# A seventh place for expert weights in a transformer block kernel: kept residuals, spent probability rows, and the order of the weight queue

## The chip, the cores and the metric

The kernel runs on one core of a Trainium2 chip (trn2). The metric is the device time of one execution in microseconds (us). The program is one hand-written instruction stream for each engine: PE (TensorE), DVE (VectorE), ACT (ScalarE), POOL (GpSimd) and SP (SyncE), which in this kernel issues most of the DMAs. The engines meet at semaphores only.

## The reference

One layer on x of 512 tokens by 1024 channels, all in float32, in three parts, each added to the residual x, and a final norm:

```python
h = rmsnorm(x, norm_mix_g);  x = x + parallel_mixers(h, ...)          # windowed attention and gated DeltaNet
h = rmsnorm(x, norm_x_g);    x = x + memory_cross_attention(h, m, ...) # 4 heads of 128, 256 memory tokens
h = rmsnorm(x, norm_ffn_g);  x = x + hierarchical_moe(h, ...)
return rmsnorm(x, norm_final_g)

# hierarchical_moe: top 1 of 4 groups, top 2 of 8 experts in it
for e in range(32):                                   # D_MODEL 1024, D_EXPERT 256
    hid = silu(t @ w_exp_gate[e]) * (t @ w_exp_up[e])
    out = out + combine[:, e:e + 1] * (hid @ w_exp_down[e])
```

The gate, up and down weights of one expert are 1024 by 256, 1024 by 256 and 256 by 1024 floats: three pieces of 1024 KB each, 96 pieces for the 32 experts.

## The kernel before, in words

The first two parts (to about 550 us of the span) are a list of jobs, `job_order()`. Every engine walks the same list and does its share of each job: PE the matmuls of a job into one of eight PSUM banks, ACT or DVE the emptying of the bank. `job_done(eng, job)` waits until PE has done a job, `job_empty(eng, job)` until its bank is emptied. `LATE_BANKS` gives fixed banks to the last jobs, and a bank is only overwritten when the job before in it was emptied. The jobs that matter here stand at the end of cross-attention and in the routing:

- `("xv", t)`: output of tile t of the attention (128 tokens). Its high part goes to `h_hi`, its low part (the rest that the rounding of the high part leaves) to `h_lo`, by a subtraction on VectorE. `("co", t, n)` multiplies both with the halves n of `w_co` and adds into the residual `xres`.
- `("rt", t)`, `("pos", t)`: router and the places of the tokens in each expert's list. `("g0", t)` gathers expert 0's rows by matmul, `("ls",)` makes the lists of rows for all experts, `("gt",)` turns expert 0's rows, `("most",)` counts the longest list.
- `("kr", h)`: a matmul with the identity that copies half a residual tile (tile 2) into PSUM, as the start of a sum.

Then comes the expert loop. Each expert has up to 64 token slots. For each, PE does: `gate_up` (64 matmuls, `bank<-arena,hT`, L1424), the turning of the next expert's gathered rows (L1411), the transpose of the hidden rows (L1446) and `down_rows` (8 matmuls, L1434). Then ACT empties the bank (L1737), and POOL scatters the rows to `y_half` in memory (L990). POOL also gathers the rows of the experts ahead (L985). Expert 31's rows are not scattered but added by matmul. After expert 30's scatter has landed, SP reads all of `y_half` back (L847, 8 reads), the tiles are summed (tiles 0 and 1 on DVE, tiles 2 and 3 in PSUM, L1507), normed and stored.

The weights live in six slots (`UNROLL`), each with a place for gate, up and down: slots 0 to 4 in the `arena` (a buffer of 32768 words for each partition) and slot 5 in the `ring` of the earlier weight chunks. Slot 2 takes words 12288 to 18431, slot 3 words 18432 to 24575, slot 4 words 24576 to 30719. The upper half of the arena is also `h_hi` (16384), `h_lo` (20480), `w_high` (24576) and `w_low` (28672), 4096 words each, while the first two parts run. So slot 3's up weights (words 20480 to 22527) lie on the first half of `h_lo`, where the low parts of the output stand until the last `co` job.

All weights are issued by SP, in one order written out by hand: the pieces of experts 0 to 5 by `load_part(b, i)` (i is 0 gate, 1 up, 2 down) between the chunks and behind `job_done` waits, and from expert 6 on by `load_expert`. That waits until the weights of the expert two before have landed (`w_loaded`, L818), until the slot's gate and up were used (`gu_done`, L819) and, ahead of the down piece, until its down was used (`down_done`, L822). The order in the queue is gate, up, down of one expert, then those of the next.

Tile 3's residual is copied to PSUM in the expert loop, behind expert 25's down (`KEEP_AT`, `keep_residual`, L1459), since `sum_banks(3)` are banks 2 and 3. The final norm's gains are loaded to the arena's last 1024 words (L841).

## Time and profile before

| what | value |
|---|---|
| time, median of 3 runs | 829.1 us (828.96 to 829.15) |
| the profiled execution | 829.2 us |
| its span, first to last instruction | 827.4 us |
| granted TensorE clock, mean | 0.994 of full speed |
| busy: PE / PE weight loads / DVE / ACT / POOL | 775.1 / 623.0 / 343.8 / 239.2 / 312.3 us |
| moved by DMA | 166.95 MB, mean 202 GB/s |
| queue of SP (q1) | 150.66 MB |
| waits of SP for landed up weights (L818), 480 us to the end | 154.7 us in 22 waits |

The page cuts the span into 40 slices of 20.7 us. All times in the rows below are microseconds from the start of the span; the profiled execution's own time is 1.8 us longer than its span. In a timeline row the first number is the start, the second the duration; x64 means that 64 instructions were merged; what stands in brackets is idle time of the engine before it, and what ended that. PEld is TensorE's weight load, SPq a DMA issue of SP.

### The profile page before, as it was taken

The numbers are of one execution on the slowest core, as the hardware profiler recorded it, in microseconds if no ns is written. First come the engines' busy times: TensorE is split into PE (matmuls) and PEld (weight loads), VectorE is DVE, ScalarE is ACT, GpSimd is POOL, SyncE is SP. The second block draws the span as 40 slices with busy tenths as digits, with TensorE's granted clock in tenths as the row PEclk, the third lists the DMA queues.
The fourth block names the chain that finished last, engine by engine and source line by source line (L and its number), as shares of the span: only waits on it lengthen the run. The fifth ranks groups of instructions, "written<-read, shape, count | busy, mean of one in ns | idle before, by whom it ended". The sixth has DMA issues, their size and how long they took to land.

```text
span 827.4 us, 14485 instructions
## 1 busy us (share of the span) xinstructions
PE 775.1 (94%) x5739; PEld 623.0 (75%) x5739; DVE 343.8 (42%) x767; ACT 239.2 (29%) x417; POOL 312.3 (38%) x354
## 2 busy tenths in 40 slices
PE   5999999999999999999999999998999999988785
PEld 5987788888988877788888887866777777756651
DVE  6466651474575484325512624372222221121126
ACT  5344242112221458632222445331111111110012
POOL 3774434542242244143542454334333333322111
PEclk9999999999999999999999999999999999999998
DMA  9956832402202232446478255679999999999976
GB/s 250 167 108 119 266 66 55 98 2 52 51 1 53 51 102 52 94 102 187 81 157 229 70 173 183 254 282 343 388 388 388 390 387 383 392 386 381 390 299 250
DMA packets 74347, 166.95 MB, mean 202 GB/s; under 512 B 18838, under 2 KB 46310, under 8 KB 66344
## 3 DMA queue, kind: packets, MB, share of 16 engines
q1 hardware_dynamic: 65856, 150.66, 57.7%
q0 software_dynamic: 5392, 9.61, 3.5%
q10 hardware_dynamic: 3032, 5.74, 2.2%
q8 instruction: 47, 0.77, 0.4%
q14 instruction: 20, 0.16, 0.1%
HBM read 157.31 MB, written 16.97 MB: 211 GB/s over the span
## 4 chain that ended last, share of the span: by engine, by line
PE 64%; DMA 25%; DVE 4%; POOL 2%; issue 2%; ACT 2%; SPq 1%; DVEq 0%; POOLq 0%; ACTq 0%
DMA arena<-in_w_exp_up 23%; PE bank L1067 15%; PE bank L1074 13%; PE bank L1076 13%; PE bank L1075 13%; PE bank L1424 2%; DMA arena<-y_half 1%; PE bank L1434 1%; PE bank L1115 1%; PE bank L1225 1%; PE bank L1167 1%; POOL w_low L889 1%; PE bank L1279 1%; POOL xres L927 1%; PE bank L1411 1%
## 5 line engine op out<-in xcount | busy, mean ns | idle before, releaser
L869 POOL TENSOR_TENSOR ring_low<-ring,w_high 128x512 fp32r<-128x512 f32 (+1 forms) x64 | 83.6, 1306 | 124.7 <-ACT w_high L1516 120.7
L1074 PE MATMUL bank<-h_hi,w_high 128*128 128x512 f32 x296 | 122.1, 412 | 0.9 <-ACT arena L1630 0.9
L1075 PE MATMUL bank<-h_lo,w_high 128*128 128x512 f32 x296 | 115.8, 391 | 0.0
L1424 PEld LDWEIGHTS bank<-arena,hT 128*64 128x64 f32 x1728 | 96.6, 136 | 24.1 <-issue 12.5
L1424 PE MATMUL bank<-arena,hT 128*64 128x128 f32 x1728 | 100.7, 274 | 8.2 <-DMA arena<-in_w_exp_up 6.1
L869 POOL TENSOR_TENSOR w_low<-ring,w_high 128x512 fp32r<-128x512 f32 x56 | 75.1, 1341 | 59.9 <-ACT w_high L1516 55.8
L2142 DVE SCALAR_TENSOR_TENSOR rt<-rt,bank 128x128 f32<-128x128 f32 x32 | 9.2, 288 | 175.2 <-ACT rt L1733 175.2
L1516 ACT ACTIVATE w_high<-ring 128x2048 fp32r<-128x2048 f32 (+1 forms) x32 | 58.9, 1839 | 57.1 <-PE bank L1076 37.2
L1074 PEld LDWEIGHTS bank<-h_hi,w_high 128*128 128x128 f32 x296 | 55.7, 188 | 15.2 <-issue 3.5
L1076 PE MATMUL bank<-h_hi,ring_low 128*128 128x512 f32 x168 | 66.1, 393 | 0.0
L1075 PEld LDWEIGHTS bank<-h_lo,w_high 128*128 128x128 f32 x296 | 55.7, 188 | 9.5
L1434 PE MATMUL bank<-arena,rt 128*64 128x512 f32 x216 | 52.3, 605 | 10.3 <-DVE rt L2146 10.3
L990 POOL DMA_INDIRECT y_half<-rows,cst x31 | 31.7, 1021 | 74.0 <-ACT rows L1737 73.2
L1074 PE MATMUL bank<-w_high,h_hi 128*128 128x512 f32 (+1 forms) x144 | 52.6, 365 | 0.5 <-DVE h_lo L2041 0.5
L1076 PE MATMUL bank<-w_high,h_lo 128*128 128x512 f32 (+1 forms) x144 | 51.2, 356 | 0.0
L1737 ACT ACTIVATE rows<-bank 128x512 f32<-128x512 f32 x32 | 19.1, 598 | 108.6 <-PE bank L1434 108.6
L1076 PE MATMUL bank<-h_hi,w_low 128*128 128x512 f32 x128 | 49.9, 390 | 0.0
L1075 PE MATMUL bank<-w_low,h_hi 128*128 128x512 f32 (+1 forms) x128 | 44.8, 350 | 0.0
L1733 ACT ACTIVATE rt<-bank 128x128 f32<-128x128 f32 x32 | 8.9, 278 | 108.2 <-PE bank L1424 105.3
L985 POOL DMA_INDIRECT hT<-h_rows,rt x31 | 30.5, 982 | 24.5 <-POOL rt L980 23.7
L1076 PEld LDWEIGHTS bank<-h_hi,ring_low 128*128 128x128 f32 x168 | 31.5, 188 | 7.4
L1516 ACT ACTIVATE arena<-bank 128x512 f32<-128x512 f32 (+1 forms) x39 | 23.3, 597 | 46.4 <-PE bank L1076 26.1
(325 smaller groups left out, 1368.7 us busy)
## 6 DMA issues: line engine op xcount, KB each, us to landing
arena<-in_w_exp_gate SPq DMA_DIRECT2D x27, 1024.0 KB
arena<-in_w_exp_up SPq DMA_DIRECT2D x27, 1024.0 KB
arena<-in_w_exp_down SPq DMA_DIRECT2D x27, 1024.0 KB
ring<-in_w_in SPq DMA_DIRECT2D x33, 512.0 KB, 6.7
ring<-in_w_exp_gate SPq DMA_DIRECT2D x5, 1024.0 KB
ring<-in_w_exp_up SPq DMA_DIRECT2D x5, 1024.0 KB
ring<-in_w_exp_down SPq DMA_DIRECT2D x5, 1024.0 KB
xres<-in_x SPq DMA_DIRECT2D x8, 512.0 KB, 7.3
```

Source lines behind the costliest of these rows:

```text
L869: after(pool.tensor_tensor(low, full, high, ALU.subtract), w_lo if kk == KD - 2 else step["pool"])
L985: pool.indirect_dma_start(out=xg[:, b % DEEP, :], out_offset=None, in_=h_rows, in_offset=bass.IndirectOffsetOnAxis(ap=idx[b][0:CAP, :], ax ...
L990: pool.indirect_dma_start(out=y_half, out_offset=bass.IndirectOffsetOnAxis(ap=at_y, axis=0), in_=ysb[:, y, :], in_offset=None, bounds_chec ...
L1067: ins = pe.matmul(o, l, r, start=(n == 0), stop=(n == len(pairs) - 1))
L1074: pe.matmul(o, l_hi, r_hi, start=(n == 0), stop=False)
L1075: pe.matmul(o, l_hi, r_lo, start=False, stop=False)
L1076: ins = pe.matmul(o, l_lo, r_hi, start=False, stop=(n == count - 1))
L1424: ins = pe.matmul(bank[CAP * half:CAP * half + CAP, 1, P * n:P * n + P], xgT[:, x, kk, :], w[:, kk, P * half:P * half + P], start=(kk == 0 ...
L1434: ins = pe.matmul(bank[CAP * half:CAP * half + CAP, o, :], hidT[:, CAP * kk:CAP * kk + CAP], down[:, kk, 512 * half:512 * half + 512], sta ...
L1516: after(nc.scalar.activation(o, i, ACT.Copy, scale=scale), s)
L1737: nc.scalar.activation(ysb[:, y, :], bank[:, 4 + b % 2, :], ACT.Copy).then_inc(y_sb, 1)
L2142: nc.vector.scalar_tensor_tensor(out=gated, in0=gate_th, scalar=1.0, in1=bank[:, 1, 0:P], op0=ALU.add, op1=ALU.mult).then_inc(step["dve"], 1)
```

## The change

- The low parts of the attention's output go to `out_lo`: the second halves of the rows of `hT` in which the probabilities of tile t stood, which `xv` no longer needs. `h_lo` is free from then on, so slot 3's up piece is issued together with its gate and down.
- Gate and up weights get seven places (`GATES = 7`), used in turn by e % 7; down weights keep six, used by e % 6. The seventh gate is in the arena's last 2048 words, the seventh up in `xres` of tiles 2 and 3.
- For that the residual of tile 3 too is copied to PSUM ahead of the expert loop: jobs `("k3", 0)` and `("k3", 1)`, banks 2 and 3, between `g0` and `ls`. `ls` moves from bank 3 to bank 5. The copy in the expert loop goes away.
- SP issues expert 6's gate right behind slot 4, its up after `k3`; and from expert 7 on the order is gate and up of expert e, then down of expert e - 1. `gu_done` is waited for one expert less, `e + 1 - 7`.
- The rows of `y_half` are read back to words 22528 to 30719 of the arena, and the final gains are loaded only after 29 experts' downs.

```diff
-KEEP_AT = {26: 3}
+GATES = UNROLL + 1
...
-    jobs += [("g0", 0), ("g0", 1), ("pos", 3), ("g0", 2), ("g0", 3), ("ls",), ("gt",), ("most",)]
+    jobs += [("g0", 0), ("g0", 1), ("pos", 3), ("g0", 2), ("g0", 3), ("k3", 0), ("k3", 1), ("ls",), ("gt",), ("most",)]
...
-LATE_BANKS = {"g0": 0, "gt": 0, "ls": 3, "most": 4, "kr": 6}
+LATE_BANKS = {"g0": 0, "gt": 0, "k3": 2, "ls": 5, "most": 4, "kr": 6}
+KEPT = ("kr", "k3")
...
+        x_row_parts = y_hi[:, :, :].rearrange("p k t -> p (k t)")
+        out_lo = [x_row_parts[:, D * t + 512:D * t + D].rearrange("p (k l) -> p k l", k=4) for t in range(NT)]
...
         def y_rows(t, j):
-            first = 2 * EW + (2 * t + j) * D
+            first = (UNROLL - 2) * EW - 2 * D + (2 * t + j) * D
...
+            n = e % GATES
+            if n < UNROLL:
+                gate, up = home(n)[:, 0:KD * FE], home(n)[:, KD * FE:2 * KD * FE]
+            else:
+                gate, up = arena[:, arena_words - KD * FE:arena_words], xres[:, 2:NT, :].rearrange("p t d -> p (t d)")
+            return [gate.rearrange("p (k f) -> p k f", k=KD), up.rearrange("p (k f) -> p k f", k=KD),
+                    home(e % UNROLL)[:, 2 * KD * FE:EW].rearrange("p (k n) -> p k n", k=2)]
...
             job_done(sp, ("cq", X_HEADS - 1))
-            load_part(3, 0)
-            load_part(3, 2)
+            for i in range(3):
+                load_part(3, i)
...
             load_part(2, 2)
-            load_part(3, 1)
             sp.wait_ge(hrow_ready, NT)
             for i in range(3):
                 load_part(4, i)
...
-                sp.wait_ge(w_loaded[(b - 2) % UNROLL], i * 32 + (32 if b >= 2 else 0))
+            load_gate(GATES - 1)
+            job_done(sp, ("k3", 1))
+            load_up(GATES - 1)
+            for e in range(GATES, EXPERTS):
+                sp.wait_ge(w_loaded[(e - 2) % UNROLL], 32 * ((e - 2) // UNROLL) + 32)
                 sp.sem_inc(loading, 1)
-                sp.wait_ge(gu_done, i * UNROLL + (b + 1 - UNROLL))
...
+                sp.wait_ge(gu_done, e + 1 - GATES)
+                load_gate(e)
+                load_up(e)
+                load_down(e - 1)
+            load_down(LAST_EXPERT)
...
+            sp.wait_ge(down_done, EXPERTS - 3)
             sp.dma_start(gain_out, norm_final_g.rearrange("(o d) -> o d", o=1).to_broadcast([P, D])).then_inc(gains_in, 16)
-            sp.wait_ge(down_done, EXPERTS - 4)
...
-                    return split_sums(o, [(h_parts(kk, slice(t * P, (t + 1) * P)), w_parts(c0, kk, 0, 512, 4)) for kk in range(4)])
+                    return split_sums(o, [(out_parts(kk, t), w_parts(c0, kk, 0, 512, 4)) for kk in range(4)])
...
-                if e1 in KEEP_AT:
-                    keep_residual(KEEP_AT[e1])
...
-                    after(tt(h_lo[s], oh4, h_hi[s].bitcast(F32), ALU.subtract), e)
+                    after(tt(out_lo[c], oh4, h_hi[s].bitcast(F32), ALU.subtract), e)
```

`load_down(e)` waits for `down_done` of `e + 1 - UNROLL`, six experts back, and issues that expert's down piece.

## Rows read from the trace of the kernel before

**Rows 1.** The page's slices of 20.7 us: GB/s moved by DMA.

```profile
GB/s 250 167 108 119 266 66 55 98 2 52 51 1 53 51 102 52 94 102 187 81 157 229 70 173 183 254 282 343 388 388 388 390 387 383 392 386 381 390 299 250
```

**Rows 2.** The page's chain that ended last: share of the span by line.

```profile
DMA arena<-in_w_exp_up 23%; PE bank L1067 15%; PE bank L1074 13%; PE bank L1076 13%; PE bank L1075 13%; PE bank L1424 2%; DMA arena<-y_half 1%; PE bank L1434 1%; PE bank L1115 1%; PE bank L1225 1%; PE bank L1167 1%; POOL w_low L889 1%; PE bank L1279 1%; POOL xres L927 1%; PE bank L1411 1%
```

**Rows 3.** Timeline of TensorE in the expert loop: gate and up (L1424), down (L1434).

```profile
575.93 1.31 PE L1424 MATMUL bank<-arena,hT 128*64 128x128 f32 x20
...
720.01 3.72 PE L1424 MATMUL bank<-arena,hT 128*64 128x128 f32 x64
...
727.57 3.77 PE L1424 MATMUL bank<-ring,hT 128*64 128x128 f32 x64 [0.18 <-DMA ring<-in_w_exp_up]
...
789.45 3.77 PE L1424 MATMUL bank<-arena,hT 128*64 128x128 f32 x64 [0.51 <-DMA arena<-in_w_exp_up]
...
794.94 1.94 PE L1434 MATMUL bank<-arena,rt 128*64 128x512 f32 x8 [0.38 <-DVE rt L2146]
...
797.56 3.52 PEld L1424 LDWEIGHTS bank<-arena,hT 128*64 128x64 f32 x64 [0.34 <-DMA arena<-in_w_exp_up]
```

**Rows 4.** Timeline of SP's DMA issues; then two rows of the page's issues.

```profile
499.02 0.33 SPq L756 DMA_DIRECT2D arena<-in_w_exp_gate  x1
...
546.24 0.38 SPq L756 DMA_DIRECT2D arena<-in_w_exp_down  x1
...
551.32 0.33 SPq L756 DMA_DIRECT2D arena<-in_w_exp_gate  x1
...
563.02 0.33 SPq L821 DMA_DIRECT2D arena<-in_w_exp_gate  x1
...
572.47 0.33 SPq L821 DMA_DIRECT2D arena<-in_w_exp_gate  x1
...
arena<-in_w_exp_up SPq DMA_DIRECT2D x27, 1024.0 KB
...
h_rows<-hT POOLq DMA_DIRECT2D x3, 512.0 KB, 3.7
```

**Rows 5.** Windows: stretch, length, busy time by engine, clock, DMA share, GB/s.

```profile
508.20:518.00 9.80, 9.30 (x56) 7.83 (x55) 3.85 (x7) 6.44 (x11) 6.29 (x6) 1.00 0.01 3
...
545.90:551.30 5.40, 5.36 (x34) 3.87 (x34) 3.78 (x18) 2.47 (x4) 2.61 (x9) 1.00 0.95 340
551.30:562.70 11.40, 8.88 (x121) 6.44 (x118) 7.44 (x39) 1.02 (x3) 2.82 (x9) 1.00 0.99 396
...
563.00:564.00 1.00, 0.00 (x0) 0.00 (x0) 0.47 (x2) 0.28 (x1) 0.80 (x2) 1.00 0.22 45
564.00:565.00 1.00, 0.46 (x3) 0.27 (x5) 0.39 (x2) 0.00 (x0) 0.41 (x1) 1.00 0.94 143
```

**Rows 6.** Timeline: tile 3's residual copy, the lists' matmuls, POOL before the first gather.

```profile
752.27 1.98 PE L1459 MATMUL bank<-xres,cst 128*128 128x512 f32 x4
754.18 2.07 PE L1424 MATMUL bank<-arena,hT 128*64 128x128 f32 x33
...
556.39 1.07 PE L1372 MATMUL bank<-cst 128*64 128x32 f32 x32
...
559.20 0.42 POOL L980 COPY rt<-rt 64x1 int32<-64x1 int32 x2 [3.56 <-DMA h_rows<-rows]
```

**Rows 7.** The chain that ended last, from expert 30's scatter on: start, duration.

```profile
798.31 4.06 DMA y_half<-rows,cst
...
806.11 9.97 DMA arena<-y_half
```

**Rows 8.** DMA queues over 564 to 604, over 801 to 802; gathers' landing times.

```profile
q1 hardware_dynamic: 2349, 13.44, 89.6%
...
q0 software_dynamic: 9, 0.02, 4.3%
q1 hardware_dynamic: 4, 0.01, 3.1%
...
DMA to landing us min/median/max: 6.6/7.1/7.4
```

More of the change, by code:

```diff
@@ L812, in _, with load_gate, load_up, load_down @@
                 load_part(4, i)
-            def load_expert(i, b):
-                parts, sources = expert_parts(b), expert_sources(i * UNROLL + b)
-                sp.wait_ge(w_loaded[(b - 2) % UNROLL], i * 32 + (32 if b >= 2 else 0))
-                sp.sem_inc(loading, 1)
-                sp.wait_ge(gu_done, i * UNROLL + (b + 1 - UNROLL))
-                for n in range(2):
-                    sp.dma_start(parts[n], sources[n]).then_inc(w_loaded[b], 16)
-                sp.wait_ge(down_done, i * UNROLL + (b + 1 - UNROLL))
-                sp.dma_start(parts[2], sources[2]).then_inc(down_loaded[b], 16)
-            for i in range(1, TURNS):
-                for b in range(UNROLL):
-                    load_expert(i, b)
-            for b in range(REST):
-                load_expert(TURNS, b)
+            def load_gate(e):
+                sp.dma_start(expert_parts(e)[0], expert_sources(e)[0]).then_inc(w_loaded[e % UNROLL], 16)
+            def load_up(e):
+                sp.dma_start(expert_parts(e)[1], expert_sources(e)[1]).then_inc(w_loaded[e % UNROLL], 16)
+            def load_down(e):
+                sp.wait_ge(down_done, e + 1 - UNROLL)
+                sp.dma_start(expert_parts(e)[2], expert_sources(e)[2]).then_inc(down_loaded[e % UNROLL], 16)
+            load_gate(GATES - 1)
[3 more added lines that the diff above has]
+                sp.wait_ge(w_loaded[(e - 2) % UNROLL], 32 * ((e - 2) // UNROLL) + 32)
+                sp.sem_inc(loading, 1)
+                sp.wait_ge(gu_done, e + 1 - GATES)
[3 more added lines that the diff above has]
+            load_down(LAST_EXPERT)
             most = sp.value_load(most_i[0:1, :], min_val=0, max_val=T)
@@ L1387, in emit @@
                     return ins
[L1388 to L1390 removed]
+                if k in KEPT:
+                    t = 2 + KEPT.index(k)
+                    job_empty(pe, ("co", t, job[1]))
+                    return pe.matmul(o, ident, xres[:, t, 512 * job[1]:512 * job[1] + 512], start=True, stop=False, skip_group_check=True)
                 if k == "most":
@@ L1396, in _ @@
             for n, job in enumerate(jobs):
-                if before_in_bank[job] and before_in_bank[job][0] not in PARTIAL + ("kr",):
+                if before_in_bank[job] and before_in_bank[job][0] not in PARTIAL + KEPT:
                     job_empty(pe, before_in_bank[job])
@@ L1416, in turn_rows, with gate_up @@
                 turn(b, turned)
-            def gate_up(b, x, s):
-                gate, up, _ = expert_parts(b)
+            def gate_up(e, x, s):
+                gate, up, _ = expert_parts(e)
                 for kk in range(KD):
@@ L1452, in expert @@
                     turn_next()
-                if e1 in KEEP_AT:
-                    keep_residual(KEEP_AT[e1])
-            def keep_residual(t):
-                for half in range(2):
-                    pe.matmul(sum_banks(t)[:, half, :], ident, xres[:, t, 512 * half:512 * half + 512], start=True, stop=False, skip_group_check=True)
             pe.sem_inc(turning, 1)
```

19 lines of the change are left out of this document (8 added, 11 removed).

## The prediction

> **What bounds the kernel now.** I read the page's row of slices first: from about 580 us to the end of the experts the DMA engines move some 390 GB/s, slice after slice, and no slice shows more; before 500 us the rate swings between nearly nothing and 270, and only then climbs [rows 1]. The chain of work that ended last then gives 23% of the span to landings of up weights, more than to any other line [rows 2]. The timeline of TensorE shows when that wait is real. An expert's gate and up matmuls start every 7.20 us from 575.93 to 720.01 (20 experts, no wait), so in that stretch TensorE sets its own pace and weights pile up ahead of it; from 727.57 on they start late, released by weights, and the gate of expert 30, which TensorE alone could have begun at 575.93 + 28 x 7.20 = 777.5, begins at 789.45 [rows 3]. So the last nine experts, and with them the end, go by the weight stream: a microsecond by which the stream is ahead at 600 us is one by which it is ahead at 790, as the engines are never idle between (the rate stays at 380 to 395) [rows 1]. TensorE has 12 us to spare. What an edit is worth is therefore: how much earlier does the stream reach the piece that the end waits for, and which piece is that.
>
> **What runs ahead of the stream.** SP issues all weights into one queue, so a piece lands in its place in the order. Slot 3's gate and down go out at 499.02, slot 5 and most of slot 2 from 518 on; slot 2's down goes at 546.24 with slot 3's up right behind it, slot 4 at 551.32, and expert 6's gate at 563.02, as soon as expert 0's gate and up matmuls let slot 0 go [rows 4]. Between, the engines idle: from 508.2 to 518 they move 3 GB/s, and after slot 4 there is a hole around 563 to 565 (45 and 143 GB/s) [rows 5].
>
> **Part 1, slot 3's up goes out with its gate.** The low parts of the output move from h_lo to rows of hT whose probabilities are spent, so one piece, 1024 KB or 1.05 MB [rows 4], leaves the stretch after 546 and falls into the idle 508 to 518: at 396 GB/s, the rate of 551.3 to 562.7 [rows 5], that is 2.65 us, costing nothing before (2.65 us fit into 9.8 idle ones). The subtraction on VectorE and the matmuls keep shape and count: 0. But slot 4 still waits for the last normed row, to 551.32. From 545.9 to 551.3 the engines moved 340 x 5.4 = 1.84 MB [rows 5]; without the piece there is only a row store of 0.52 MB [rows 4] and 1.05 of slot 2's down in that queue, 1.57, so it runs dry 0.27 MB, or 0.7 us, before 551.3: at 550.6. A load takes time to flow: in the 2 us after the issue at 563.02 only 0.19 MB moved, worth 0.5 us, so 1.5 are lost [rows 4, 5]. Slot 4 flows from 551.3 + 1.5 = 552.8. A new hole of 2.2 us; net gain 2.65 - 2.2 = 0.45.
>
> **Part 2, the seventh gate and up.** They are issued right behind slot 4, before expert 0 has run, and close the old hole: the queue was dry at 562.7 and flowed again at 563.0 + 1.5 = 564.5, 1.8 us. So the stream is ahead by 0.45 + 1.8 = 2.25, say 2.3 us. Not by the 5.3 us that two pieces of 1.05 MB take: the stream can gain only time in which it stood still. The bounds: if slot 4 follows without a hole of its own, 2.65 + 1.8 = 4.5; if the new hole is as large as the piece and latency is 1 us, 0 + 1.3 = 1.3.
>
> **Part 3, tile 3's residual moves ahead of expert 0.** The same four matmuls took from 752.27 to the next start at 754.18, 1.9 us, in a place where the weights were late anyway [rows 3, 6]; taking them away there gives 0. In their new place, between the first gather's sums and the slot lists, TensorE has no idle time (the lists' matmuls begin at 556.39 with no wait) [rows 6], so lists, first gate and all experts start 1.9 us later. TensorE's 12 us of slack cover that at the end. What is late next is the issue of gate 7 (564.9 instead of 563.0), of down 6 behind expert 0's down, and of gate 8 (572.47 + 1.9 = 574.4) [rows 4]. Queued then: slot 4 until 562.2, after it five pieces, 5.24 MB; the queue's own rate among gathers is 13.44 MB in 40 us, 336 GB/s [rows 8], so 15.6 us, to 577.8. It isn't dry at 574.4: 3.4 us of cover, and 0 for this part. Without that cover it would cost up to 1.9. The gathers wait for the lists too; the last row store already held them to 559.20 [rows 6], so they lose under 1.2 us. The ls bank (5) was emptied by then.
>
> **Part 4, the order of the pieces.** Before: gate, up, down of one expert. After: gate 31, up 31, then down 30, down 31. In mid-stream nothing changes. At the end the critical step is expert 30's down: its result must be scattered to memory and read back, and the chain goes from its start at 794.94 to the last read at 816.09 [rows 3, 7]. It began 5.5 us after up 30 landed, and its own weights, the next piece, were there by then. Now down 30 stands last but one in the queue, the place of up 31 before, and up 31 was waited for to 797.56 [rows 3]. So without a gain down 30 would start at 797.5: a loss of 2.6 us (bounds 2.3, as the weight load was held only the last 0.34 us, and 2.9, one piece of 2.65 us behind a down that comes late by 0.3). With 2.3 us of lead it starts at 795.2, +0.3 to now. TensorE could start it at: down 29 in up 30's old place, 789.4 - 2.3 = 787.1, plus 1.9 for it, 3.7 for gate and up, 1.7 for hidden: 794.4, so the weights decide.
>
> **Part 5, the scatter behind it.** It took 4.06 us from 798.31 [rows 7], with weights still in the engines: between 801 and 802 nine of its packets ran beside four of the weight queue [rows 8]. Now the weights end 2.3 us before it: those nine come with the others. I take 0.7 us off, between 0 (it is bound by its own start and end) and 1.4 (all the time after 801). By the Trainium skill (DMA: Bandwidth & Descriptors, Anatomy of one DMA) such a transfer takes about 2.0 us plus bytes over 436 GB/s; for 128 rows of 2 KB that is 2.6 us, against 4.06 in the trace, and by it the gain would be 1.4 and the sum 828.0 in place of 828.7. The first gathers contend as before. The final gains load (0.5 MB) is issued after expert 28 instead of at the last weights: it stays behind down 31 in the queue, and nothing asks for it before the tiles are summed: 0. Reads of y into other words of the arena: 0, their slots are free after expert 28, and SP waits for the scatter far longer.
>
> **Sum.** On the profiled 829.2: order +2.6, lead -2.3, scatter -0.7, rest 0: 828.8; against the median of 829.1 that is 828.7. Its own range, with the lead at 1.8 to 3.0 and the scatter at 0.3 to 1.2, is 827.4 to 829.6. About 0.2%, 1.7 us, is what a measurement here tells from no change.
>
> **Rivals.**
> (a) The lead is larger than the holes I count: slot 4 without a new hole (the piece in front still fills the time, as row stores drag) gives 4.5, and the scatter 1.0: 829.1 + 2.6 - 4.5 - 1.0 = 826.2; with the low order cost 825.9. For it: the rate of 545.9 to 551.3 is only 340, so something slows pieces there. Against it: the engines' share is 0.95 in it, so they are held, not idle [rows 5], and SP issues at fixed waits. It is over the bound from a lead of 3.6. Chance 0.28.
> (b) Slower: expert 0's delay of 1.9 us becomes a hole. If queue time is shorter than I think, or the first gathers land late (they take 6.6 to 7.4 us) [rows 8], SP stands at gate 8 or down 7 with an empty queue. Lead 2.3 - 1.9 = 0.4, order +2.6, scatter 0: 829.1 + 2.2 = 831.3. It decides from a lead plus scatter under 0.9. For it: down 6 and the first gathers all fall in the 10 us behind the gate at 563.02, where SP's waits and TensorE's steps stand closest [rows 4]. Against it: the 3.4 us of cover. Chance 0.2.
> (c) The seventh place does nothing for the stream because the w_loaded wait (two experts back) limits it. Then lead 0.45 and order 2.6: 830.6 after the scatter; this is within the bound. In the trace that wait first binds past 600 us. It shares the 0.52 of the middle with my forecast, 0.07 of it.
>
> **Numbers.** Forecast 0.45 and (c) 0.07 make 0.52 within 0.2%; (a) 0.28 faster; (b) 0.20 slower. The range goes from (a)'s 826.2 to just short of (b)'s, 831.0.
>
> **What would show it.** In the new profile: SP issues slot 3's up near 499.4 and the engines are busy to 511; a hole at 550.6 to 552.8 and none at 563 (step 1, 2); the first expert's gate 1.9 us later (3); past 740 us TensorE waits in front of L1434's down matmuls for in_w_exp_down, no more for in_w_exp_up, and expert 30's down starts near 795.2 (4); scatter to landing near 3.4 us (5). Wrong it would be if the last down 30 landed more than 1.5 us off 795.2, or if a second hole stood between 565 and 600.

## Result and the profile after

The changed kernel takes 831.03 us (median of 20 executions, 829.2 to 834.1) against 829.18 for the kernel before (20 executions on the same chip, 828.5 to 830.7): a ratio of 1.0023 with a 95% interval of 1.0016 to 1.0029. It is 1.9 us slower; I had forecast 828.7 with 831.0 as the upper end and gave "slower" 2 chances in 10. The profiled execution took 829.5 us (span 827.6), which is at the fast end of the changed kernel's executions, so its trace shows the places of the loss and not its full size. The executions also scatter more than before (standard deviation 1.25 us against 0.62), and their mean granted TensorE clock lies between 0.981 and 0.991: the lower the clock, the longer the execution as a rule (correlation -0.65 over the 20).

The page's slices and chain, which answer to [rows 1] and [rows 2]: the slices after 580 us look the same, and the chain now has landings of down weights in it, which it had not.

```profile
GB/s 250 167 108 120 265 67 54 100 1 52 51 2 52 51 102 52 95 101 186 81 151 231 73 172 234 254 227 365 374 389 379 396 389 385 388 386 389 392 289 248
...
DMA arena<-in_w_exp_up 16%; PE bank L1080 15%; PE bank L1087 13%; PE bank L1089 13%; PE bank L1088 13%; DMA xres<-in_w_exp_up 4%; PE bank L1441 3%; DMA arena<-in_w_exp_down 2%; DMA ring<-in_w_exp_up 2%; PE bank L1451 1%; PE bank L1517 1%; PE bank L1131 1%; PE bank L1241 1%; DVE h_lo L1830 1%; PE bank L1295 1%
```

SP's issues (timeline of SP; to be held against [rows 4]) and windows of the changed kernel (against [rows 5]; columns as there):

```profile
499.60 0.43 SPq L765 DMA_DIRECT2D arena<-in_w_exp_up  x1
...
551.60 0.33 SPq L765 DMA_DIRECT2D arena<-in_w_exp_gate  x1
...
558.79 0.33 SPq L826 DMA_DIRECT2D xres<-in_w_exp_up  x1
...
578.91 0.33 SPq L823 DMA_DIRECT2D arena<-in_w_exp_gate  x1
```

```profile
508.20:518.00 9.80, 9.30 (x56) 7.84 (x56) 3.92 (x8) 6.65 (x11) 6.16 (x5) 1.00 0.27 110
...
551.30:554.00 2.70, 1.61 (x8) 0.29 (x4) 2.23 (x13) 0.27 (x1) 0.33 (x1) 1.00 0.38 52
...
563.00:565.00 2.00, 2.00 (x41) 2.00 (x39) 1.32 (x8) 0.00 (x0) 1.19 (x3) 1.00 1.03 426
...
579.00:581.00 2.00, 1.62 (x11) 1.10 (x12) 1.31 (x4) 0.20 (x1) 0.23 (x2) 1.00 0.82 158
```

Slot 3's up goes out at 499.60 and falls into the idle stretch (110 GB/s where 3 were). The old hole at 563 is closed (426 GB/s). The new hole that I had placed at 550.6 to 552.8 stands at 551.3 to 554, with 52 GB/s. A second one, which I had ruled out and named as a sign of being wrong, stands at 579 to 581 (158 GB/s). Gate 8, which waits for expert 1's gate and up to be used, goes out at 578.91, where I had written 574.4. In the kernel before, the issue that waited for the same matmuls was gate 7's, at 572.47.

TensorE's timeline shows why, and then the late experts (k3's copy is L1407, lists L1388, gate and up L1441, turn L1428, down L1451; against [rows 3, 6]):

```profile
556.77 1.98 PE L1407 MATMUL bank<-xres,cst 128*128 128x512 f32 x4
558.69 1.12 PE L1388 MATMUL bank<-cst 128*64 128x32 f32 x32
...
561.60 3.74 PE L1441 MATMUL bank<-arena,hT 128*64 128x128 f32 x64 [1.06 <-DVE hT L2104]
...
567.40 3.53 PE L1451 MATMUL bank<-arena,rt 128*64 128x512 f32 x8 [0.38 <-DVE rt L2156]
571.54 1.07 PE L1428 MATMUL bank<-cst,hT 64*128 64x64 f32 x8 [0.61 <-DMA hT<-h_rows,rt]
573.48 5.40 PE L1441 MATMUL bank<-arena,hT 128*64 128x128 f32 x64 [0.87 <-DMA arena<-in_w_exp_up]
...
762.87 3.26 PE L1451 MATMUL bank<-arena,rt 128*64 128x512 f32 x8 [2.43 <-DMA arena<-in_w_exp_down]
...
781.17 1.94 PE L1451 MATMUL bank<-arena,rt 128*64 128x512 f32 x8 [2.69 <-DMA arena<-in_w_exp_down]
...
788.64 1.94 PE L1451 MATMUL bank<-ring,rt 128*64 128x512 f32 x8 [0.68 <-DMA ring<-in_w_exp_down]
790.38 3.71 PE L1441 MATMUL bank<-arena,hT 128*64 128x128 f32 x64
...
796.60 1.94 PE L1451 MATMUL bank<-arena,rt 128*64 128x512 f32 x8 [1.17 <-DMA arena<-in_w_exp_down]
```

Expert 0's gate comes 2.35 us later than before (561.60 against 559.25), of which 0.28 stood already when slot 4 was issued (551.60 against 551.32); the copy itself pushes it by 2.07. Its down matmuls take 3.53 us where they took 1.94, and expert 1's gate and up 5.40 where they took 3.74. (The wait in brackets there is put down to up weights, but the same 0.88 us stands there in the kernel before, released by VectorE.) Those are the stretches with half the granted clock, 1.2 instead of 2.4 GHz:

```profile
568.00:571.00 3.00, 2.93 (x8) 0.49 (x4) 0.00 (x0) 0.03 (x1) 0.00 (x0) 0.50 0.99 268
574.50:577.50 3.00, 3.00 (x32) 3.00 (x31) 0.00 (x0) 0.00 (x0) 1.33 (x3) 0.50 0.99 404
```

The turn of expert 1 (571.54) waits for gathers, which take longer now (landing times of the gathers issued in 555 to 575; in the kernel before they are 7.2/7.3/7.4 in the same window):

```profile
DMA to landing us min/median/max: 6.7/9.1/9.4
```

At the other end the waits in front of gate and up have turned into waits in front of down. Expert 30's down starts at 796.60 (before 794.94; I had written 795.2). The chain of the end, start and duration, and below it the timeline of the scatter (L1003) and the reads (L860), against [rows 7]:

```profile
778.64 17.82 DMA arena<-in_w_exp_down
796.60 1.94 PE bank L1451 x8
799.13 3.71 PE bank L1441 x64
```

```profile
799.96 0.99 POOL L1003 DMA_INDIRECT y_half<-rows,cst  x1 [6.78 <-ACT rows L1747]
...
802.42 4.22 SPq L860 DMA_DIRECT2D arena<-y_half  x8
```

From the scatter's start to the first read it is 2.46 us, where it was 4.13 (798.31 to 802.44). So the reads start at 802.42, as early as before, although expert 30's down is 1.7 us later.

### The profile page after: what moved, and what is told of

Same layout as the page of the kernel before. It is cut to its first block, busy times and chain, and to the rows that moved or that the text cites. A ratio compares the mean times of both kernels' runs of the same rounds, so it can differ in the third digit from the quotient of the medians.

```text
span 827.6 us, 14484 instructions
## 1 busy us (share of the span) xinstructions
PE 777.7 (94%) x5739; PEld 626.4 (76%) x5739; DVE 344.6 (42%) x767; ACT 239.6 (29%) x417; POOL 310.2 (37%) x354
## 4 chain that ended last, share of the span: by engine, by line
PE 65%; DMA 24%; DVE 5%; ACT 2%; POOL 1%; issue 1%; SPq 1%; DVEq 0%; ACTq 0%; POOLq 0%
DMA arena<-in_w_exp_up 16%; PE bank L1080 15%; PE bank L1087 13%; PE bank L1089 13%; PE bank L1088 13%; DMA xres<-in_w_exp_up 4%; PE bank L1441 3%; DMA arena<-in_w_exp_down 2%; DMA ring<-in_w_exp_up 2%; PE bank L1451 1%; PE bank L1517 1%; PE bank L1131 1%; PE bank L1241 1%; DVE h_lo L1830 1%; PE bank L1295 1%
## 5 line engine op out<-in xcount | busy, mean ns | idle before, releaser
L882 POOL TENSOR_TENSOR ring_low<-ring,w_high 128x512 fp32r<-128x512 f32 (+1 forms) x64 | 81.7, 1277 | 126.6 <-ACT w_high L1526 122.7
L1441 PEld LDWEIGHTS bank<-arena,hT 128*64 128x64 f32 x1664 | 97.9, 138 | 17.0 <-issue 16.0
L1441 PE MATMUL bank<-arena,hT 128*64 128x128 f32 x1664 | 104.9, 276 | 1.9 <-DVE hT L2104 1.1
L1451 PE MATMUL bank<-arena,rt 128*64 128x512 f32 x216 | 55.2, 634 | 15.9 <-DVE rt L2156 8.4
L1003 POOL DMA_INDIRECT y_half<-rows,cst x31 | 31.7, 1021 | 76.6 <-ACT rows L1747 75.7
L1451 PEld LDWEIGHTS bank<-arena,rt 128*64 128x64 f32 x216 | 14.0, 141 | 37.3 <-issue 21.8
L1089 PE MATMUL bank<-w_high,h_lo 128*128 128x512 f32 (+1 forms) x112 | 38.7, 345 | 0.0
```

Of the source, the lines that this page charges most:

```text
L882: after(pool.tensor_tensor(low, full, high, ALU.subtract), w_lo if kk == KD - 2 else step["pool"])
L1003: pool.indirect_dma_start(out=y_half, out_offset=bass.IndirectOffsetOnAxis(ap=at_y, axis=0), in_=ysb[:, y, :], in_offset=None, bounds_chec ...
L1089: ins = pe.matmul(o, l_lo, r_hi, start=False, stop=(n == count - 1))
L1441: ins = pe.matmul(bank[CAP * half:CAP * half + CAP, 1, P * n:P * n + P], xgT[:, x, kk, :], w[:, kk, P * half:P * half + P], start=(kk == 0 ...
L1451: ins = pe.matmul(bank[CAP * half:CAP * half + CAP, o, :], hidT[:, CAP * kk:CAP * kk + CAP], down[:, kk, 512 * half:512 * half + 512], sta ...
```

## Experiments

Each was run beside the kernel before on the same chip, and the ratio is to that kernel. "Interval" is the 95% one. A trace is of one execution, which can lie over 2 us from the median; where it does, I say so.

**1. The old order from expert 16 on, the rest as changed.**

```diff
                 load_gate(e)
                 load_up(e)
-                load_down(e - 1)
-            load_down(LAST_EXPERT)
+                if e <= 16:
+                    load_down(e - 1)
+                if e >= 16:
+                    load_down(e)
```

> The changed kernel, but from expert 16 on the queue has the old order again (gate, up, down of one expert); the seventh place stays. Theory A (the order at the end costs what the lead gains: in the profile of the changed kernel expert 30's down waits for its weights until 796.6): the critical down starts 5.5 us after up 30, which now lands in down 29's place less one piece, near 788.3, so at 793.9 in place of 796.6, and the time falls by 2 to 2.7 us against the changed kernel, to about 828.5, faster than the kernel before by 0.1%. Theory B (the order is free, all of the loss is made ahead of 600 us by late gathers and the low clock): no change to the changed kernel, 831.0.

Measured: 829.63 us, 1.0006, interval 0.9997 to 1.0014. So the new order costs the changed kernel 1.4 us, and everything else in the change together is worth nothing, +0.5 us, where I had counted -2.3. The gain is real but short of theory A's 2 to 2.7 us. The trace is of the slowest of the 11 executions (830.96), so it can't show the gain: gate 30 starts at 790.99 and down 30 at 796.47. The early stage is as in the changed kernel, somewhat worse (timeline of TensorE; turn L1430, gate and up L1443), and 39 GB/s move over 579 to 581:

```profile
571.48 1.07 PE L1430 MATMUL bank<-cst,hT 64*128 64x64 f32 x8 [2.55 <-DMA hT<-h_rows,rt]
573.42 6.60 PE L1443 MATMUL bank<-arena,hT 128*64 128x128 f32 x64 [0.88 <-DMA arena<-in_w_exp_gate]
```

**2. Tile 3's copy behind expert 0's gate and up, the rest as changed** (up 6 then goes out behind gate and up 7).

```diff
-... ("g0", 3), ("k3", 0), ("k3", 1), ("ls",) ...
+... ("g0", 3), ("ls",) ...
-            job_done(sp, ("k3", 1))
-            load_up(GATES - 1)
...
+                if e == GATES:
+                    sp.wait_ge(kept, 1)
+                    load_up(GATES - 1)
...
                 gate_up(e1 - 1, b % 2, gu_done)
+                if e1 == 1:
+                    for half in range(2):
+                        ins = pe.matmul(sum_banks(3)[:, half, :], ident, xres[:, 3, 512 * half:512 * half + 512], start=True, stop=False, skip_group_check=True)
+                    ins.then_inc(kept, 1)
```

> The changed kernel, but tile 3's residual is copied to PSUM behind expert 0's gate and up, where TensorE idles 1.35 us for the hidden rows, and expert 6's up is issued behind expert 7's gate and up. Theory B (the copy on TensorE's path delays lists, gathers and expert 0, and with them SP's issues): first gate at 559.6 in place of 561.6, gate 8 issued 2 us earlier or more, the hole near 579 smaller, the time 1 to 2 us less than the changed kernel's 831.0. Theory A': the delay of the gathers comes from weights in front of them in the DMA engines, and not from the copy: turning of expert 1's rows stays near 571, gain under 0.5 us.

Measured: 829.84 us, 1.0016, interval 1.0005 to 1.0027. Expert 0's gate is back at 559.44, the gathers at 6.6/7.7/8.3 us, and in this trace expert 1's gate and up take 3.74 us at full clock; down 30 starts at 796.07. The clock is not the edit's doing, though: run 5 below has the same code up to expert 13, and there they take 5.40 us. Gate 8 goes out at 577.80, only 1.1 us earlier than in the changed kernel, as SP now waits 9.8 us for the landing of up 6, which stands further back in the queue. The time improves by 0.07% only, where theory B had 1 to 2 us, and the intervals do not tell it from nothing. What becomes of the rest isn't shown; the late stage of this trace has three down matmuls of 3.1 to 3.7 us in place of 1.94.

**3. The copy ahead of the lists alone**, on the kernel before (six places, old order, `ls` in bank 5).

```diff
-... ("g0", 3), ("ls",) ...
+... ("g0", 3), ("k3", 0), ("k3", 1), ("ls",) ...
-LATE_BANKS = {"g0": 0, "gt": 0, "ls": 3, "most": 4, "kr": 6}
+LATE_BANKS = {"g0": 0, "gt": 0, "k3": 2, "ls": 5, "most": 4, "kr": 6}
-KEEP_AT = {26: 3}
+KEEP_AT = {}
...
```

> The kernel before, but tile 3's residual is copied to PSUM ahead of the lists as in the changed kernel, and no longer behind expert 25; six places and the old order stay. Theory B: the stream waits for expert 0's gate, so SP's gate 6 goes out 1.9 to 2.3 us later, all of it shows at the end: 831.2, slower by 0.25%. Theory A: the stream makes good for it (no idle in the engines counts), within 0.5 us of 829.2.

Measured: 830.23 us, 1.0012, interval 1.0003 to 1.0021: 1.0 us for two microseconds of matmuls whose end I had priced at 0. Gate 0 starts at 561.31 (2.06 later), gate 6 goes out at 565.08 instead of 563.02, and down 30 starts at 797.62. Theory B had twice as much (+2.0 us).

**4. Slot 3's up early alone** (with the low parts in `out_lo`), on the kernel before.

```diff
-            load_part(3, 0)
-            load_part(3, 2)
+            for i in range(3):
+                load_part(3, i)
...
             load_part(2, 2)
-            load_part(3, 1)
```

> The kernel before with only the low parts of the output in the probability rows and slot 3's up issued with its gate; six places, old order, old residual copy. By my sum the piece brings 2.65 us and the new hole ahead of slot 4 takes 2.2 of it: 828.7, a gain of 0.45. The rival (no new hole, the piece in front drags) gives 2.6 us, 826.5. In the profile of the changed kernel the engines are empty from 551.0 to 553.6, which speaks for a hole of 2.6 and a gain near 0.

Measured: 828.34 us, 0.9987, interval 0.9978 to 0.9996: 1.1 us faster. Gate 30 starts at 788.94 and down 30 at 794.43, each 0.5 us earlier than before, as the sum of part 1 had it (0.45). The time gains more than that, but its interval reaches down to 0.3 us.

**5. Both repairs: old order from expert 13 on (as in 1, with 13 for 16), and the late copy (as in 2)**, seven places.

> The changed kernel with both repairs: tile 3's residual copied behind expert 0's gate and up (expert 6's up issued behind expert 7's), and the old order of the queue from expert 13 on. If the loss is made of the order at the end (1.4 us by the first pair of runs) and of the copy on TensorE's path (0.6 us), the two add up: 829.0 or less, near the low parts alone (828.3), and with the seventh place's own worth on top (a hole of 1.8 us closed) up to 827.5. Rival: the seventh place itself is worth nothing, as its loads stand in front of the first gathers: then no better than the low parts alone, 828.3.

Measured: 828.23 us, 0.9986, interval 0.9977 to 0.9994. Better than the changed kernel by 0.37%, but no better than part 1 alone: the seventh place, with the late copy that makes room for it, gives nothing here. Windows of part 1 alone (first fence) and of this kernel (second):

```profile
551.30:554.00 2.70, 1.43 (x8) 0.27 (x4) 2.24 (x13) 0.09 (x1) 0.14 (x1) 1.00 0.57 99
563.00:565.00 2.00, 0.45 (x5) 0.18 (x3) 0.86 (x3) 0.28 (x1) 1.20 (x3) 1.00 0.71 160
...
565.00:570.00 5.00, 4.12 (x38) 2.63 (x40) 0.69 (x1) 0.60 (x1) 1.28 (x4) 1.00 0.98 380
575.00:580.00 5.00, 5.00 (x73) 4.08 (x70) 0.00 (x0) 0.82 (x2) 1.81 (x3) 1.00 1.02 400
```

```profile
563.00:565.00 2.00, 2.00 (x10) 0.89 (x7) 0.57 (x2) 0.28 (x1) 1.20 (x3) 1.00 1.03 403
...
565.00:570.00 5.00, 3.35 (x18) 1.45 (x17) 0.70 (x2) 0.60 (x1) 0.45 (x2) 1.00 0.98 302
575.00:580.00 5.00, 4.62 (x46) 2.98 (x43) 1.46 (x4) 0.74 (x2) 1.36 (x3) 1.00 1.02 329
```

The hole at 563 is closed (403 against 160 GB/s over 2 us, 0.49 MB), but the stream gives it back: in 565 to 570 and 575 to 580 the engines are just as busy and move 0.39 and 0.36 MB less. From 546 to 605 us SP's queue moves 18.24 MB, and 18.38 in part 1 alone. Expert 1's gate and up take 5.40 us at low clock in this trace; but in run 2's, where they take 3.74, the same two stretches move 320 and 318 GB/s, so the loss is not the clock's.

**6. The new order alone**, on the kernel before (six places).

```diff
                 for n in range(2):
                     sp.dma_start(parts[n], sources[n]).then_inc(w_loaded[b], 16)
-                sp.wait_ge(down_done, i * UNROLL + (b + 1 - UNROLL))
-                sp.dma_start(parts[2], sources[2]).then_inc(down_loaded[b], 16)
+                e = i * UNROLL + b
+                if e > UNROLL:
+                    load_down(e - 1)
+                if e == LAST_EXPERT:
+                    load_down(e)
...
```

> The kernel before with only the new order of the queue from expert 7 on (down of an expert behind the next gate and up); six places, all else old. Theory A with the clock: expert 30's down waits for its weights at up 31's old place, 797.5 in place of 794.94, the scatter behind it shorter by 1.6: +1.0 us; and as TensorE now waits in front of down, its clock falls to 0.5 in some experts past 730 us, more than once an execution: mean clock 0.987 to 0.990 in place of 0.9956, spread of the runs 1.2 us in place of 0.6, in all +1.0 to +2.0 us, 830 to 831. Rival: the low clock comes from the early stage alone: clock 0.995, spread 0.6, +1.0 us at most.

Measured: 832.59 us (5 executions), 1.004, interval 1.0027 to 1.0053: 3.3 us slower. Timeline of TensorE at the end (gate and up L1431, down L1441):

```profile
755.00 3.59 PE L1441 MATMUL bank<-arena,rt 128*64 128x512 f32 x8 [1.77 <-DMA arena<-in_w_exp_down]
...
782.63 3.42 PE L1441 MATMUL bank<-arena,rt 128*64 128x512 f32 x8 [2.65 <-DMA arena<-in_w_exp_down]
...
791.31 1.94 PE L1441 MATMUL bank<-ring,rt 128*64 128x512 f32 x8 [0.38 <-DVE rt L2153]
798.52 1.94 PE L1441 MATMUL bank<-arena,rt 128*64 128x512 f32 x8 [0.38 <-DVE rt L2153]
```

Down 30 (798.52) waits for no weights: behind the wait of 2.65 us and a down of 3.42 us at low clock (0.72 over 782 to 788), TensorE goes at its own 7.2 us an expert to the end.

Not all of the 3.3 us is the order at the end. With six places the edit also moves down 6 behind gate 7 and up 7, which wait for expert 1, and so it opens an early hole (the window below moved 343 GB/s in the kernel before):

```profile
570.00:575.00 5.00, 4.62 (x58) 3.56 (x56) 1.46 (x4) 0.28 (x1) 1.84 (x3) 1.00 0.70 191
```

From 499 to 605 us SP's queue moves 26.46 MB against 27.19, which at 390 GB/s is 1.9 us. The changed kernel hasn't got this hole, so run 6 doesn't price the order in it.

**7. Slot 4's gate issued ahead of the wait for the last normed row**, on kernel 5.

```diff
             load_part(2, 2)
+            load_part(4, 0)
             sp.wait_ge(hrow_ready, NT)
-            for i in range(3):
+            for i in range(1, 3):
                 load_part(4, i)
```

> As the run with both repairs, and slot 4's gate is issued right behind slot 2's down, ahead of the wait for the last normed row, so that the queue doesn't run dry between 551 and 553.6. Theory: the stream is ahead by up to 2.6 us more, and the end with it, 1 to 2.6 us under the run with both repairs. Rival: the last row store and the first gathers wait behind that piece by as much, expert 1's rows are turned 2 us later, and SP loses at gate 8 what it won: no gain, within 0.5 us.

Measured: 827.10 us, 0.9974, interval 0.9964 to 0.9984; run again beside 13 below, 827.32 us, 0.9978, interval 0.9969 to 0.9987. It beats both kernels, by 2 us the one before and by nearly 4 the changed one. The windows show the hole of 551 filled, and the one of 563 open again (107 GB/s), since behind gate 6 nothing goes out before gate 7 at 563.1:

```profile
551.30:554.00 2.70, 1.42 (x8) 0.25 (x4) 2.24 (x13) 0.07 (x1) 0.13 (x1) 1.00 1.00 381
563.00:565.00 2.00, 2.00 (x7) 0.82 (x5) 0.57 (x2) 0.28 (x1) 1.20 (x3) 1.00 0.63 107
```

The gathers land after 6.8 us, expert 1's turn starts at 567.36 with no wait and its gate takes 3.74 us; gate 30 starts at 786.91, down 30 at 792.40.

**8. Matmuls in the waits**, on the changed kernel: three 128x128 matmuls in front of the wait for down weights, from expert 20 on, so that TensorE does not stand still there.

```diff
                 pe.wait_ge(y_sb, e1)
+                if e1 > 20:
+                    for _ in range(3):
+                        pe.matmul(bank[:, 4 + b % 2, 0:P], ident, ident, start=True, stop=True, skip_group_check=True)
                 pe.wait_ge(down_loaded[b], 16 * i + 16)
```

> The changed kernel with three small matmuls (128 by 128, about 0.3 us each, into the bank that the down matmuls overwrite next) in front of the wait for the down weights, from expert 20 on: work that nobody reads, so that TensorE doesn't stand still there. If the low clock in these waits is what the new order costs and spreads: no 0.5 in the late windows, spread of the runs back to 0.7, median 0.5 to 1.5 us under the changed kernel's 831.0. Rival: the clock plays no part, only the weights' place in the queue: no change or +0.5 us, and the same spread.

Measured: 833.81 us, 1.0049, interval 1.0037 to 1.0061. A miss: the three matmuls take 0.94 us, an expert 8.07 instead of 7.20, and that made TensorE the bound. It shows nothing on the clock at the end.

**9. The same for experts 26 to 30 only.**

> The changed kernel with the same three small matmuls in front of the wait for the down weights, but for experts 26 to 30 alone, where the profile of the changed kernel shows waits of 0.68 to 2.69 us there. In the run before, from expert 20 on, they took 0.87 us of each expert and made TensorE the bound (a start every 8.07 us). Theory (the low clock in the last experts costs and spreads): median 0.5 to 1 us under the changed kernel, ratio 1.001 to 1.002, no 0.5 past 760 us. Rival (place in the queue only): the fillers cost up to 1 us, ratio 1.003 to 1.004.

Measured: 831.16 us, 1.0022, interval 1.001 to 1.0033: no change that the interval shows. It doesn't decide between the two: the interval holds all of the theory's range (1.001 to 1.002) and the lower end of the rival's (1.003). The trace is of the fastest of the 12 executions (828.65, 2.5 us under the median). In it there is no low clock from 766 to 800, and down 30 starts at 795.87 with no wait, 0.7 earlier than in the changed kernel; but the added matmuls again make TensorE the bound there (8.07 us an expert). The trace is of more use for the early stage, which is the changed kernel's. Expert 1's gate and up run at full clock in it, and there is no second hole (L1441, and window):

```profile
573.13 3.74 PE L1441 MATMUL bank<-arena,hT 128*64 128x128 f32 x64 [0.88 <-DMA arena<-in_w_exp_up]
579.00:581.00 2.00, 2.00 (x20) 1.06 (x18) 0.13 (x1) 0.42 (x1) 1.12 (x2) 1.00 1.02 410
```

**10. Six places, part 1 and slot 4's gate early** (kernel 4 with the edit of 7).

> The run with the low parts alone (six places, old order, old residual copy), and slot 4's gate issued ahead of the wait for the last normed row. Theory: with six places the stream must wait for expert 0's gate (563.0) in any case; what the hole at 551 wins is lost in front of 563, so no gain over the low parts alone: 0.9987, within 0.0006. Rival: the seventh place is worth nothing and the hole at 551 is all: 0.9974 as in the run with seven places.

Measured: 829.15 us, 0.9994, interval 0.9986 to 1.0003. So the early gate does not pay by itself, and with seven places it does (0.9974): the seventh place, with its late copy, is worth about 0.2% once the hole of 551 is filled (run 11 below, on the same chip, has 0.9974 as well). With six, the hole only moves (182 GB/s over 558 to 563), and SP issues nothing until 563.29.

**11. All of slot 4 ahead of the wait**, on kernel 5.

> The run with both repairs, and all three pieces of slot 4 ahead of the wait for the last normed row (its gate alone gave 0.9974). Theory: the hole was closed by one piece; two more only stand in front of the row store that the first gathers wait for, up to 5 us: the gathers land later, expert 1's rows are turned after 570 in place of 567.4, SP's next issues come late: 1 to 2 us worse than with the gate alone, 0.9985 to 1.0. Rival: the stores share the engines with the weights and aren't held: the same 0.9974.

Measured: 827.31 us, 0.9974, interval 0.9963 to 0.9984; the gathers take 7.3 us. As good as 7; the longer queue does not hold the row store and gathers enough to matter.

**12. The new order to the end, on kernel 7.**

> The fastest so far (both repairs and slot 4's gate early), but with the new order of the queue to the end. The early stage is the same, so the order alone speaks: expert 30's down waits for its weights; 2.6 us later less 1.6 of a shorter scatter gives +1.0, and the low clock in front of down another 0.5 to 1.5: ratio 0.9990 to 1.0005 against 0.9974, spread 1.2 us, mean clock 0.988. Rival: the order costs nothing where the stream is ahead: 0.9974.

Measured: 829.35 us, 1.0000, interval 0.9991 to 1.001: the order costs 2.2 us on a base where expert 1 runs at full clock and no second hole stands before 600 us. Its late stage (gate and up L1445, down L1455):

```profile
786.89 3.21 PE L1455 MATMUL bank<-ring,rt 128*64 128x512 f32 x8 [1.03 <-DMA ring<-in_w_exp_down]
789.83 4.20 PE L1445 MATMUL bank<-arena,hT 128*64 128x128 f32 x64
...
795.76 1.94 PE L1455 MATMUL bank<-arena,rt 128*64 128x512 f32 x8 [0.38 <-DVE rt L2164]
```

**13. The same, but expert 30's down ahead of gate 31 and up 31**, beside kernel 7 once more. This takes the last down's late place away and leaves the waits in front of the downs before it.

```diff
+                if e == LAST_EXPERT:
+                    load_down(e - 1)
                 load_gate(e)
                 load_up(e)
...
-                load_down(e - 1)
+                if e < LAST_EXPERT:
+                    load_down(e - 1)
             load_down(LAST_EXPERT)
```

> The seventh-place kernel with the late copy and slot 4's gate early, in the new order (gate and up, then the down before) up to expert 30, but at the very end expert 30's down goes ahead of gate 31 and up 31; nothing else differs from the run with the new order to the end, which stood at 1.0000 of the kernel before, where the old order stood at 0.9974. Theory of the place in the queue: what the order costs is that expert 30's down stands behind gate 31 and up 31. Then this change alone gives back the 2.2 us, down 30 starts about as early as with the old order (gate 30 near 787 to 790, down 30 near 792 to 793, at its own pace), and the ratio is 0.997 to 0.998. Theory of the clock: the waits in front of the downs of experts 25 to 29 stay, with granted clock 0.5 behind them (down matmuls of 3.2 to 3.6 us in place of 1.94), and TensorE reaches gate 30 late, at 789.5 or after; then the ratio stays at 0.999 to 1.000 and the mean clock under 0.991.

> The fastest kernel so far again (late copy, slot 4's gate early, old order of the pieces from expert 13 on), beside the run above on the same chip. Both theories: 0.997 to 0.998 of the kernel before, mean granted clock over 0.993, gate 30 near 787 and down 30 near 792.4; it is the yardstick for the ratio of the other.

Measured: 828.49 us, 0.9992, interval 0.9982 to 1.0002, mean clock 0.989 (old order beside it: 827.32, 0.9978, clock 0.994). The time is in the range of the theory of the clock and so is the mean clock, and down 30 starts 2 us later than the other theory had it; but the trace gives another cause than the clock. Its end (gate and up L1448, down L1458), then that of kernel 7 run beside it (L1446, L1456):

```profile
770.96 2.46 PE L1458 MATMUL bank<-arena,rt 128*64 128x512 f32 x8 [2.90 <-DMA arena<-in_w_exp_down]
773.14 4.94 PE L1448 MATMUL bank<-arena,hT 128*64 128x128 f32 x64
...
787.63 1.94 PE L1458 MATMUL bank<-ring,rt 128*64 128x512 f32 x8 [0.87 <-DMA ring<-in_w_exp_down]
789.37 3.71 PE L1448 MATMUL bank<-arena,hT 128*64 128x128 f32 x64
...
794.81 1.94 PE L1458 MATMUL bank<-arena,rt 128*64 128x512 f32 x8 [0.38 <-DVE rt L2167]
```

```profile
787.09 3.77 PE L1446 MATMUL bank<-arena,hT 128*64 128x128 f32 x64 [0.35 <-DMA arena<-in_w_exp_up]
...
792.58 1.94 PE L1456 MATMUL bank<-arena,rt 128*64 128x512 f32 x8 [0.38 <-DVE rt L2165]
```

The piece that ends the wait lands at nearly the same time, 787.6 and 787.1: it is the same place in the queue. In the old order it is up 30 and releases gate 30 at once; in the new order it is down 29, and its matmuls (1.74 us to the next start) come first. So gate 30 and down 30 start 2.2 us later, with the clock at full speed there: the low clock behind 770.96 had been made up by the waits after it. The scatter gives back 1.2 of the 2.2: to the first read it is 2.46 us where the weights have nearly ended (798.18 to 800.64) and 3.63 beside them (795.95 to 799.58).

## Why the prediction was wrong

**The sum by its terms.** The runs split the measured +1.9 us so, on one path: parts 1 and 2 without the early copy -1.2 (run 5), the early copy +1.7 (run 5 to run 1, 0.9986 to 1.0006), the order together with the scatter +1.4 (run 1 to the changed kernel). On the other path the order comes first, +2.5 (run 5 to run 2), and then the early copy, +0.6 (run 2 to the changed kernel). So the two don't simply add: the copy is worth 0.6 to 1.7 us, the order 1.4 to 2.5. I had -2.3 for the lead, 0 for the copy and +1.9 for order and scatter. The first two were off, and both on the side of too fast; the differences between runs of separate occasions carry some 0.1% of uncertainty each.

**Part 3 is the step that failed** ("It isn't dry at 574.4: 3.4 us of cover, and 0 for this part"). The queue ran dry about when I had it: 577.8 in the sum, and in the trace the engines' rate falls from 410 GB/s in 577 to 578 to 246 in the microsecond behind it. Wrong was the 574.4. I carried the copy's delay to gate 8 as 572.47 + 1.9, but it grows on its way, in two steps. Four of the traces have the changed kernel's early code (the changed kernel itself, runs 1, 8 and 9); the last columns are what SP's queue moved from 499 to 605 us, and what that is ahead of the kernel before (27.19 MB) at 390 GB/s:

| trace | expert 1's gate and up: start, length | gate 8 issued | GB/s, 579 to 581 | MB | ahead |
|---|---|---|---|---|---|
| run 9 | 573.13, 3.74 us | 576.90 | 410 | 27.97 | 2.0 us |
| changed kernel | 573.48, 5.40 us | 578.91 | 158 | 27.39 | 0.5 us |
| run 8 | 573.32, 6.62 us | 579.97 | 70 | 26.99 | -0.5 us |
| run 1 | 573.42, 6.60 us | 580.05 | 39 | 26.93 | -0.7 us |

The first step is in all four. The gathers take 8.7 to 9.4 us (median) instead of 7.3, expert 1's turn waits for them, and its gate starts 4.4 to 4.8 us later than before (568.70), not 1.9. By itself that brings gate 8 to 576.90, still inside the cover: run 9 has no hole, and its lead of 2.0 us is near the 2.3 of the sum. The second step is the clock. In the other three the granted clock falls to 0.5, expert 1's gate and up take 5.40 to 6.62 us, gate 8 goes out as soon as they end, and the queue is dry by then: 1.5 to 2.7 us of lead are gone. The prediction has neither step in its sum. Rival (b) names the first, late gathers and an empty queue at gate 8; that its 831.3 lies so near the measured 831.03 is luck, since it had no gain from the scatter and nothing of the clock.

Two limits to this. Why the gathers take 9 us is not shown: without the early copy, and with a queue that doesn't pause either, they take 7.7 and 7.9 (runs 2 and 5), and with the copy and six places, where the queue does pause (82 GB/s over 563 to 565), 3.8 (run 3). And what lets the clock fall in one execution and not in the next is open: it fell in run 5 and not in run 2, which are the same up to expert 13. There gate 8 waits for the landing of up 6 (577.80 and 578.12), the wait that rival (c) names, and it opens no hole: the engines' share is 0.98 to 1.02 over 575 to 585. That the copy costs something without clock and second hole is shown by run 3, 1.0 us, interval 0.2 to 1.7 us.

**Parts 1 and 2, the size of the lead.** This is the second term that failed. The mechanism of part 1 was right (a new hole of 551 to 554), and down 30 came 0.5 us earlier with it alone, as worked out; the time improved by 1.1 us. The 1.8 us of part 2 was mis-sized: with the hole at 563 closed, nothing was gained in time (run 5 against 4). I counted a closed hole as lead without asking what the stream does next: at the same busy share the engines move 302 and 329 GB/s where they had moved 380 and 400. That this is the gathers of experts 1 and 2, which now run beside the weights, is my reading; no run takes them away. Only when slot 4's gate also fills the hole of 551 does the seventh place pay, about 0.2% (runs 7, 10 and 11). In the trace of the changed kernel the lead at the end is 797.5 - 796.46 = 1.0 us (down 30 landed at 778.64 + 17.82) in place of 2.3. That is 1.3 us off my 795.2, inside the 1.5 that I had allowed; the sign that came was the second hole.

**Part 4, the order.** The waits moved in front of the downs as foretold, and the net of parts 4 and 5 was about right: +1.9 forecast, 1.4 to 2.5 in the changed kernel and 2.2 on the base of kernel 7 (all with the faster scatter in them). The reason I gave covers only part of it. Run 13 shows that 1.2 us remain when down 30 has its old place, and where they are: the weights of down 29 stand where up 30 stood, and its matmuls lie between their landing and gate 30. I had that path in one line ("TensorE could start it at ... 794.4") and set it aside, since the weights came 0.8 us later; with both paths within a microsecond, taking either away gives little. The other 0.7 to 1.0 us (0.9992 to 1.0000, on separate occasions) is down 30's place or low clock; in run 12's trace it is the clock, since down 30 starts without a wait for weights behind a down of 3.21 and a gate and up of 4.20 us. How it divides in the median execution stays open: the filled waits of runs 8 and 9 did not tell, and a trace is of one execution.

**Part 5, the scatter.** I took 0.7 off; it was 1.7 (4.13 to 2.46, start to first read), past my upper bound of 1.4. By the Trainium skill (DMA: Bandwidth & Descriptors, Anatomy of one DMA) its 128 rows take an estimated 2.6 us; the trace comes within 0.2 of that once the weights have nearly ended, and beside them it is far off. But the profile shows only 0.14 MB moved by this scatter, not the 0.26 MB of 128 rows. It made up for the late down 30 and did not bring the end forward: expert 31's matmuls and the sums behind them, from 799.13 on, are now the chain that ends last.

**The spread of the executions.** Every kernel with the new order has a mean clock of 0.987 to 0.991, those with the old one 0.9925 to 0.996; a start without the second hole does not change it (runs 2, 12 and 13 have it, and are at 0.987 to 0.989). In these traces the clock falls behind most of the waits of 1.0 to 2.9 us in front of down. In the nine traces of the old order the waits of 1.0 to 2.3 us in front of gate and up are mostly followed by full clock; it fell behind four of them (2.01 us in run 3, 2.22 to 2.31 in runs 7, its repeat and 11). That this makes the longer executions is likely, but no run took the low clock away alone.

## What to carry to other kernels

A delay of work that issues later loads must be followed through everything it meets (gathers that share the engines, the engine's clock, the next waits) and not added once at the end; a cover of 3.4 us was spent by a delay of 2. Where executions of one kernel differ, compare the traces of several before a hole is put down to an edit. Closing an idle stretch in a queue is a gain only if the queue is not held further on: test the closing of each hole together with the next. In a queue of weights, ask for each piece what must be computed between its landing and the last critical step: a piece in the same place that must be used before the next is worth its own matmuls in time.

## What the runs showed of the hardware

- Eight down matmuls take 1.94 us at the full clock; behind waits of 1.0 to 2.7 us for weights they took 3.1 to 3.7 in many places, and the granted clock is low there (0.72 over 782 to 788 of run 6). It isn't each such wait: 2.69 us at 781.17 of the changed kernel was followed by 1.94, and 2.43 at 762.87 by 3.26. Two executions of the same early code can differ in it (expert 1's gate and up 3.74 us in run 2, 5.40 in run 5).
- The first gathers issued by POOL land after 3.8 us (median) in run 3, where the weight queue pauses, after 6.8 to 7.9 in runs 2, 5, 7 and 11, and after 8.7 to 9.4 in the four traces with the changed kernel's early code.
- Expert 30's scatter takes 3.6 to 4.4 us beside the weight stream (4.06 before, 3.61 in the repeat of run 7, 4.41 in run 10) and 2.4 to 2.5 once it has nearly ended.
- Between the issue of a load into a dry queue and full flow, some 2 us pass: slot 4's gate goes out at 551.60, 25 and 66 GB/s move in the next two microseconds, and 340 from 554 to 555.
